# Two token-mixing stages: suffix sums that run on in one bank, score products in fours, values in pairs, another split of the PSUM banks and another order

## The reference, cut to what matters

```
proj = h @ w_in                       # 1024 -> 3072 columns: q, k, v of three kinds of heads
o_a  = chunk_band_attention(...)      # 6 band heads, 64 wide
o_b  = diff_attention(...)            # 4 differential heads: two softmax maps each, queries and keys 32 wide
o_c  = stick_breaking_attention(...)  # 6 stick-breaking heads, 64 wide
y    = concat(o_a, o_b, o_c) @ w_out
```

```
log_one_minus = where(strict, log_sigmoid(-z), 0)
suffix = cumsum(log_one_minus, reverse=True) - log_one_minus
a = where(strict, exp(log_beta + suffix), 0)
```

## Time and profile before

| | us |
|---|---|
| median of 3 runs | 2588.81 (2588.8 to 2589.32) |
| the profiled execution | 2589.32 |
| its span in the profile | 2587.5 |
| TensorE matmul busy | 2560.7 (99%) |
| VectorE, ScalarE, GpSimd busy | 1637.7, 1169.8, 423.3 |
| the `MIX_ORDER` part of the first mixing (981.8 to 1245.3) | 263.5 |
| granted TensorE clock | full in all slices but the first |

### The profile page before, as it was taken

How to read it: one execution, slowest core, us unless ns; L and a number is a source line. 1 busy time by engine, 2 the same in 40 slices (tenths; PEclk the granted TensorE clock), 3 DMA queues, 4 the chain that set the end, 5 groups by cost and what they waited for, 6 DMA issues and landing times.

```text
span 2587.5 us, 42242 instructions
## 1 busy us (share of the span) xinstructions
PE 2560.7 (99%) x17332; PEld 2222.2 (86%) x17332; DVE 1637.7 (63%) x2667; ACT 1169.8 (45%) x2019; POOL 423.3 (16%) x416
## 2 busy tenths in 40 slices
PE   9999999999999999999999999999999999999998
PEld 7788887678999888867899988999888876899987
DVE  3425653667999353456699735899444356699833
ACT  4123333643655234465455533555334456355522
POOL 0230010001332011111143200233001020133200
PEclk9999999999999999999999999999999999999999
DMA  8722140012333232211233332332323212223321
GB/s 323 290 93 93 38 123 33 34 58 82 99 106 107 98 117 67 66 50 66 82 115 100 113 114 66 115 115 98 114 82 104 64 50 83 66 90 115 115 96 67
DMA packets 183854, 252.73 MB, mean 98 GB/s; under 512 B 13040, under 2 KB 158448, under 8 KB 179184
## 3 DMA queue, kind: packets, MB, share of 16 engines
q1 hardware_dynamic: 183664, 250.04, 29.0%
HBM read 247.92 MB, written 2.10 MB: 97 GB/s over the span
## 4 chain that ended last, share of the span: by engine, by line
PE 92%; DVE 3%; ACT 2%; issue 1%; DMA 1%; POOL 1%; SPq 0%; POOLq 0%; ACTq 0%; DVEq 0%
PE psum L816 89%; PE psum L1384 1%; DMA mod_w<-in_l_ab_w_mod 1%; PE psum L1268 1%; PE psum L884 1%; DVE stats_first L2206 0%; DVE work L2199 0%; ACT w_hi L1558 0%; DVE X L2202 0%; ACT work L1606 0%; POOL stats_first L2925 0%; PE psum L860 0%; DVE h_lo L2138 0%; DVE wide L2236 0%; POOL stats L2980 0%
## 5 line engine op out<-in xcount | busy, mean ns | idle before, releaser
L816 PE MATMUL psum<-h_hi,w_hi 128*128 128x256 f32 (+1 forms) x1520 | 498.2, 328 | 0.4 <-DVE w_lo L2105 0.3
L816 PE MATMUL psum<-h_lo,w_hi 128*128 128x256 f32 (+1 forms) x1520 | 490.9, 323 | 0.0
L816 PE MATMUL psum<-h_hi,w_lo 128*128 128x256 f32 (+1 forms) x1520 | 490.8, 323 | 0.0
L2105 DVE TENSOR_TENSOR w_lo<-raw,w_hi 128x2048 fp32r<-128x2048 f32 (+1 forms) x99 | 223.4, 2260 | 295.1 <-ACT w_hi L1558 294.6
L816 PEld LDWEIGHTS psum<-h_hi,w_hi 128*128 128x128 f32 x1520 | 290.0, 191 | 32.6 <-issue 9.7
L816 PEld LDWEIGHTS psum<-h_hi,w_lo 128*128 128x128 f32 x1520 | 289.6, 191 | 22.6
L816 PEld LDWEIGHTS psum<-h_lo,w_hi 128*128 128x128 f32 x1520 | 289.9, 191 | 20.0 <-issue 0.5
L1558 ACT ACTIVATE w_hi<-raw 128x2048 fp32r<-128x2048 f32 (+1 forms) x100 | 188.5, 1888 | 259.5 <-PE psum L816 249.5
L816 PE MATMUL psum<-w_hi,ff_hi 128*128 128x512 f32 x576 | 225.2, 391 | 1.2 <-DVE ff_lo L2722 1.2
L816 PE MATMUL psum<-w_lo,ff_hi 128*128 128x512 f32 x576 | 224.4, 390 | 0.0
L816 PE MATMUL psum<-w_hi,ff_lo 128*128 128x512 f32 x576 | 224.4, 390 | 0.0
(11 more groups left out here) (364 smaller groups left out, 5444.4 us busy)
## 6 DMA issues: line engine op xcount, KB each, us to landing
raw<-in_ffn_w_gate SPq DMA_DIRECT2D x44, 1024.0 KB, 5.2
raw<-in_ffn_w_up SPq DMA_DIRECT2D x44, 1024.0 KB, 5.2
raw<-in_ffn_w_down SPq DMA_DIRECT2D x44, 1024.0 KB, 4.7
raw<-in_w_in SPq DMA_DIRECT2D x36, 512.0 KB, 5.0
raw<-in_l_ab_w_in SPq DMA_DIRECT2D x10, 1024.0 KB, 9.3
mod_w<-in_l_ab_w_mod SPq DMA_DIRECT2D x8, 1024.0 KB, 17.9
raw<-in_w_out SPq DMA_DIRECT2D x8, 1024.0 KB, 4.8
raw<-in_cd_w_in SPq DMA_DIRECT2D x7, 1024.0 KB, 5.3
```

What stands on the lines that cost most here:

```text
L816: return pe.matmul(o, lhsT, rhs, start=start, stop=stop, skip_group_check=True)
L2105: dve.tensor_tensor(lo[:, 0:nk * n], raw[c % 2][:, 0:nk * n], hi[:, 0:nk * n].bitcast(F32), ALU.subtract).then_inc(*w_lo_made.mark(key))
```

## The change

1. **Suffix sums.** The key tiles are taken from the last to the first, all of a head in one bank (`("csum", s, h)`). After tile `kt+1` has been read by VectorE, a product with `strict` (its sum with `suffix_tri` is all ones) completes that tile's columns to a full sum, and the triangle product of tile `kt` is added. So `stick_sums` has a product over `strict` (128, 256, 384 wide) in place of those over `ones`, and it waits for VectorE's step before.
2. **Scores of differential heads.** `diff_quad` makes the four maps of two heads one behind the other, at rows 0, 32, 64, 96, in four banks.
3. **Values.** `band_value_pair` and `diff_value_pair` make two heads' values in one bank, side by side.
4. **Banks.** Projections have bank 0 alone, band and differential heads 1 to 5, stick-breaking heads 6 and 7; `widen` comes late.
5. **Order.** All four strings are new.
6. **Feed-forward.** S3 and S4 move from GpSimd to VectorE (`last_mixed`), behind the rests of A1 and A22 and ahead of the other rests.

```diff
-    streams["a"] = [step for i in range(0, len(bands), 2) for step in [("band_pair", *streams["a"][i][1:]), *streams["a"][i:i + 2]]]
+    for letter, both in (("a", "band_pair"), ("c", "band_value_pair"), ("d", "diff_quad"), ("g", "diff_value_pair")):
+        single = streams[letter]
+        streams[letter] = [step for i in range(0, len(single), 2) for step in [(both, *single[i][1:]), *single[i:i + 2]]]
-                           [("stick_sums", h, kt) for kt in range(NT)] + ...
+                           [("stick_sums", h, kt) for kt in reversed(range(NT))] + ...
 MIX_LETTERS = {
-    "pe": ("vppspspsaapbpbppppappbbppppcpcappppppppppcbcppcppttbppssbpdtpptppdfppadpssppsppcpppbpspspsfbpccpppabppppcppdpbafbdpppppc"
-           "ssgttgttpffgdpcsspdpppcsdfspspspbbppgappppfdggfdppdfpfdgpgpppfcdggppfdgcstbfdbggastfdccttssfabbsccabbgnfgccbbpcpaogcppnp"
-           "pppppnbobppppppccooprpppnpppppppprppppr"),
+    "pe": ("pppappabpbpapppcbppppspbsppspapppppcbbppppbcpppbtapptspptppdspppppcpbpppfptppsppabppspppabppcspfbpspsdgspbbppapppppctp"
+           "pppfdtpfptgdspfpspsftpsppppsbfcgspdspsfbvppcgpdfpfppdapfttsgstfstsbbcafgnsbpbpafocppgabpbppnpdcopppbbppfpfnogcppppprpn"
+           "pppproppppppppr"),
...
-                proj, soft, stick = Ring([0, 1]), Ring([2, 3, 4]), Ring([5, 6, 7])
+                proj, soft, stick = Ring([0]), Ring([1, 2, 3, 4, 5]), Ring([6, 7])
...
+                    elif kind == "band_value_pair":
...
+                        for odd in range(2):
+                            pe.wait_ge(*probs_turned["a", s, i + odd])
+                            done(attend(v_a, h + odd, t, b, turned["a"][(i + odd) % 2]), ("av", s, i + odd))
...
+                    elif kind == "diff_quad":
...
+                        banks = [claim(soft.take(), ("bs", s, i + n // 2, n % 2)) for n in range(4)]
...
+                        for n, b in enumerate(banks):
+                            p0 = 32 * n
+                            done(mm(bank(b, width), q_b[p0:p0 + 32, h // 2, t * P:(t + 1) * P], k_b[p0:p0 + 32, h // 2, 0:width], True, True),
+                                 ("bs", s, i + n // 2, n % 2))
...
                     elif kind == "stick_sums":
...
-                        m = mm(bank(b, L - kt * P), tri[:, :], soft_[:, STARTS[kt]:STARTS[kt] + L - kt * P], True, kt == 3)
-                        for k2 in range(kt + 1, NT):
-                            m = mm(bank(b, L - k2 * P, (k2 - kt) * P), ones[:, :], soft_[:, STARTS[k2]:STARTS[k2] + L - k2 * P], False, k2 == 3)
+                        if kt == NT - 1:
+                            claim(stick.take(), ("csum", s, h))
...
+                        else:
+                            pe.wait_ge(*stick_dve["sums", s, h, kt + 1])
+                            mm(full(("csum", s, h), L - (kt + 1) * P, (kt + 1) * P), strict[:, 0, :], soft_[:, STARTS[kt + 1]:STARTS[kt + 1] + L - (kt + 1) * P],
+                               False, False)
+                        m = mm(full(("csum", s, h), L - kt * P, kt * P), tri[:, :], soft_[:, STARTS[kt]:STARTS[kt] + L - kt * P], kt == NT - 1, kt == 0)
...
                 first_mixed(keys[0])
                 for name in ("A1", "A22"):
                     lo_blocks(keys[0], name)
+                last_mixed(keys[0])
...
-                        for q, key in enumerate(fast_keys(s[1], layer)):
-                            mixed_ = {name: fast_weights(key, name)[2] for name in ("S1", "S2", "S3", "S4")}
...
-                            pool.tensor_tensor(mixed_["S3"], fast_block(key, 0, 0), fast_block(key, 0, 1), ALU.subtract).then_inc(*fast_mixed.mark((key, "S3")))
```

More of the change, by code:

```diff
@@ L189, in mix_streams @@
                            ([("stick_part", h, part) for part in range(3)] + [("stick_scores", h)]) * (letter == "s") + [("stick_abs", h), ("stick_log", h), ("stick_mask", h)] +
-                           [("stick_sums", h, kt) for kt in range(NT)] + [("stick_exp", h)] + [("stick_value_pair", h)] * (letter == "s") +
+                           [("stick_sums", h, kt) for kt in reversed(range(NT))] + [("stick_exp", h)] + [("stick_value_pair", h)] * (letter == "s") +
                            [("stick_values", h)]]
@@ L245 @@
 BAND_ITEM = {(step[2], step[3]): step[1] for step in MIX_ORDER["dve"] if step[0] == "band_scores"}
-DIFF_ITEM = {(step[2], step[3]): step[1] for step in MIX_ORDER["pe"] if step[0] == "diff_scores"}
+DIFF_ITEM = {(step[2], step[3]): step[1] for step in MIX_ORDER["dve"] if step[0] == "diff_scores"}
 def build(nc, A, out):
@@ L1433, in mixing @@
                         turn_probs(("at", s, i), band_slot(i), t)
-                    elif kind == "band_values":
+                    elif kind == "band_value_pair":
                         _, i, h, t = step
                         b = claim(soft.take(), ("av", s, i))
+                        bank_of["av", s, i + 1] = b
                         if h in (0, 4):
                             pe.wait_ge(*mix_kept[s, "v", int(h == 4), t])
-                        pe.wait_ge(*probs_turned["a", s, i])
-                        done(attend(v_a, h, t, b, turned["a"][i % 2]), ("av", s, i))
-                    elif kind == "diff_scores":
+                        for odd in range(2):
+                            pe.wait_ge(*probs_turned["a", s, i + odd])
+                            done(attend(v_a, h + odd, t, b, turned["a"][(i + odd) % 2]), ("av", s, i + odd))
+                    elif kind == "diff_quad":
                         _, i, h, t = step
                         width = (t + 1) * P
[L1444 to L1449, removed]
+                        banks = [claim(soft.take(), ("bs", s, i + n // 2, n % 2)) for n in range(4)]
+                        if t == 0:
+                            pe.wait_ge(*mix_kept[s, 1408 + P * (h // 2)])
+                        for n, b in enumerate(banks):
+                            p0 = 32 * n
+                            done(mm(bank(b, width), q_b[p0:p0 + 32, h // 2, t * P:(t + 1) * P], k_b[p0:p0 + 32, h // 2, 0:width], True, True),
+                                 ("bs", s, i + n // 2, n % 2))
                     elif kind == "diff_turn":
@@ L1453, in mixing @@
                         turn_probs(("bt", s, i), map0[i % 2], t)
-                    elif kind == "diff_values":
+                    elif kind == "diff_value_pair":
                         _, i, h, t = step
                         b = claim(soft.take(), ("bv", s, i))
+                        bank_of["bv", s, i + 1] = b
                         if h == 0:
                             pe.wait_ge(*mix_kept[s, "v", 3, t])
-                        pe.wait_ge(*probs_turned["b", s, i])
-                        done(attend(v_b, h, t, b, turned["b"][i % 2]), ("bv", s, i))
+                        for odd in range(2):
+                            pe.wait_ge(*probs_turned["b", s, i + odd])
+                            done(attend(v_b, h + odd, t, b, turned["b"][(i + odd) % 2]), ("bv", s, i + odd))
                     elif kind == "stick_part":
@@ L2037, in mixing @@
                         event = ("bv", s, i)
-                        copy(o_tok[:, t, 384 + h * 64:384 + (h + 1) * 64], event, full(event, 64), attn_kept, (s, i), scale=stat("diff", i, 6, 7))
+                        act.wait_ge(*psum_full["bv", s, i | 1])
+                        copy(o_tok[:, t, 384 + h * 64:384 + (h + 1) * 64], event, full(event, 64, 64 * (h % 2)), attn_kept, (s, i), scale=stat("diff", i, 6, 7))
+                        freed["bv", s, i - h % 2] = attn_kept[s, i]
                     elif kind == "stick_scores":
@@ L2056, in mixing @@
                         z = stick_ring[h % 2][1]
-                        act.wait_ge(*stick_dve["sums", s, h, 3])
+                        act.wait_ge(*stick_dve["sums", s, h, 0])
                         act.activation(z[:, :], z[:, :], ACT.Exp).then_inc(*stick_step.mark(("weights", s, h)))
@@ L2671, in first_mixed, with last_mixed @@
                     dve.tensor_tensor(s2, s1, fast_block(key, 0, 0), ALU.subtract).then_inc(*fast_first.mark((key, "S2")))
+                def last_mixed(key):
+                    s2, s3, s4 = (fast_weights(key, name)[2] for name in ("S2", "S3", "S4"))
+                    dve.tensor_tensor(s3, fast_block(key, 0, 0), fast_block(key, 0, 1), ALU.subtract).then_inc(*fast_mixed.mark((key, "S3")))
+                    dve.wait_ge(*fast_first[key, "S2"])
+                    dve.tensor_tensor(s4, fast_block(key, 1, 0), s2, ALU.subtract).then_inc(*fast_mixed.mark((key, "S4")))
                 def half_sums(q):
@@ L2748, in ffn @@
                         lo_blocks(following, "A22")
+                        last_mixed(following)
                     else:
```

42 lines of the change are left out of this document (17 added, 25 removed).

## The result

The changed kernel takes 2556.05 us (median of four runs, 2555.84 to 2556.28), the kernel before 2589.07 on the same chip. The ratio is 0.9872, 95% interval 0.9855 to 0.9889. The direction was right, and 13.8 us of gain were not foreseen (in the spans, 2554.5 us where the sum gave 2568.3).

What follows compares the result with a forecast made beforehand. TensorE, busy 99% of the span, was taken as the bound; 2587.5 - 25.2 (10.6 + 11.7 + 2.9) + 6.0 = 2568.3 us of span, 2569.6 us predicted time, range 2557 to 2583.

Steps and rivals of the forecast that it cites:

- Suffix sums: TensorE's stick-breaking sums in the mixings: `strict` replacing `ones` saves 0.88 us a head, 10.6 us in both layers.
- Quads: TensorE's differential scores: four maps in one step cost as much as two, saving 11.7 us in both layers.
- quads in twos: Rival for differential scores: third and fourth row groups wait, the 11.7 us gain falls away, 2581.3 us; chance 0.10.
- Feed-forward at nothing: Key loop: S3 and S4 add 1.2 us a key to VectorE, regained from GpSimd's absence; 0 us, bounds 0 and 5.
- The last rival: VectorE becomes the bound in feed-forward, 0.5 us over TensorE a key, 36 us, 2605.6 us; chance 0.03.
- New waits, +6 us: TensorE's waits in the mixings for the one projection bank and VectorE's subtractions: 3 us a layer; bounds minus 5, plus 20.
- The bank's 0.6: Waits at new projections' claims of the one bank, 27 a layer, with ScalarE free: 0.6 us a layer.
- The doubling: The sum of new waits doubled to 3 us a layer because ScalarE and VectorE aren't always free.
- Values: TensorE's value products in the mixings: 13 more neighbours a layer at 0.11 us, 2.9 us saved in both; bounds 1.6, 4.2.
- 53 to 55, nothing: Stretches of TensorE's dense work, each with a switch at both ends, go from 53 to 55, which costs nothing.
- The late chain: Rival: TensorE waits for a stick-breaking pair's scores-to-mask chain, 3 us at two pairs a layer, 12 us, 2581.6; chance 0.13.

Runs made afterwards that it cites:

- z2: The changed kernel with eight attention steps a layer, standing at claims of the projection bank, moved behind the next projection's first piece; 2574.31 us against 2556.22 unaltered.
- y1: The changed kernel with one additional full-array product between the two heads' products of each value pair, 40 in all; 2569.82 us.
- y2: The changed kernel with the same kind of additional full-array product ahead of each value pair, 40 in all; 2561.36 us.
- v3: The changed kernel with VectorE's split of chunk 10's weights moved behind two band scores, one step of band values and two of differential weights; 2555.88 us.
- y4_swap: The changed kernel with one exchange in TensorE's order, `(4, 3)` before `(5, 2)` at the end of heads 5 and 4; 2560.29 us against 2556.22 unaltered.

## Why the prediction fell short, by its own steps

- Suffix sums: right (10.6 forecast, 10.5 given back).
- Quads: right in sum (11.7; 11.6 to 11.8 by the distances, up to 12.8 by the time) and in the mechanism: 1.07 us for a quad of 512. The rival "quads in twos" fell, and had it been true it would have cost 6.7 us, not 11.7. The Trainium skill (TensorE: Matmul & The Clock Gate, Part 3: Packing small matmuls) has four row tiles at 3.07 times the speed of one after the other, and the prediction's estimate from it was 1.12 us. This trace nearly agrees: 1.07.
- Feed-forward at nothing: right, and for the stated reason, GpSimd's company. The last rival fell with it. VectorE's load didn't stay, as the prediction had it, but fell by 10 us in 194. (A key is 84 x 194.0/1566 = 10.4 us there and not 10.1; nothing hangs on it.)
- **New waits, +6 us: the step that failed.** The prediction let the 2.7 us of old idle time stand in each layer and added 3. The trace has 2.5 in all, so the term was -0.3: 6.3 of the 13.8 us. Two things were wrong in it. Of the 3 us, 1.9 came: 0.45 for `(5, 2)`, foreseen at 0.5, and 0.55, 0.62 and 0.23 for two late masks and a copy of scores, which the sum didn't have. The bank's 0.6, doubled, came to nothing: every claim had a cover longer than its copy, and eight bare ones cost 18 us (z2). The doubling had no row behind it. And of the old 2.7 some 2 us went with the new order, about 4 in both layers. That is the larger part; the range had it in its low end, the sum did not.
- **Values and "53 to 55, nothing": mis-sized.** I counted stretches of dense work, where the array's changes of shape had to be counted. In the two traces the entries from full-array products into small shapes fall from 52 to 38 in the first mixing. A change there and back costs 0.28 us (y1, y2), and the sum had the 0.10 of it that lies on the small step. The other 0.18, at 14 places in both layers, is 5.0 us that the sum left out. This is an estimate: no run undoes those entries alone, and the price of 64-column products is taken for scores as well.
- **A hidden wait in the kernel before.** Its last score pair 512 columns wide took 1.90 us, where the prediction priced it at 1.06. First TensorE (the pair, then a narrower window of it), then VectorE:
```profile
1174.50 1.98 PE L816 MATMUL psum<-k_b,q_b 32*128 32x512 f32 x4
1176.40 1.15 PE L816 MATMUL psum<-v_a,work 128*64 128x64 f32 x32
...
1175.35 1.12 PE L816 MATMUL psum<-k_b,q_b 32*128 32x512 f32 x2
```
```profile
1174.28 1.02 DVE L2874 TENSOR_TENSOR log_weights<-log_weights,psum 128x384 f32<-128x384 f32 x2 [2.18 <-PE psum L816]
```
By the old string the second map takes the bank of a suffix sum, which VectorE reads until 1175.30; the map starts at 1175.35 and runs behind the first instead of beside it. No idle time is recorded, since the first map was still running. The second mixing has the same at 2161.60. In the changed kernel no quad is longer than its usual time. That is 0.84 us a layer, 1.7 in both, in no term of the sum.
- The late chain, forecast as a rival of 12 us: it exists, at 0.55 and 0.62 us at two places a layer in the changed kernel, within the 2.5 us of idle.
- Still open: 13.8 - 6.3 - 5.0 - 1.7 = 0.8 us. Of these terms the 5.0 is an estimate, and the other two are read from traces of two kernels whose orders differ. No experiment divides them, and single parts of the change in the old order weren't tried.

## What to carry to other kernels

When one buffer replaces two, list for each claim what stands between the last use and the next, and compare it with the copy: if every cover is longer, as at the 27 claims here, no wait is left for a second buffer to save (no run gave the second bank back in the new order); but moving a few steps then costs a good part of the gain. Price a small-shaped product with the steps ahead of it and behind it, not only from its own start. Don't take the old idle time for a constant when the order changes, and look for waits in steps that are longer than their likes, not only in idle time. And look for the engine that ended 0.1 us before a wait's end before trusting the name on the wait.

## What the hardware showed that was not expected

- The granted clock of TensorE fell behind close waits. In the changed kernel 0.45 and 0.62 us of idle within 2.5 us left it at 1.00. In v3 the same pair (0.45 and 0.61) was followed by 0.66 over 2125 to 2130, at the second mixing only; in y4_swap one wait of 1.98 us was followed by 0.66 over 1155 to 1160. In such a stretch a pair of 128x256 sums took 0.86 us from start to start instead of 0.43: half speed, the lower level of 1.2 GHz, for some 3 us, which costs 1.4. Runs of one kernel differ by about this much (2554.69 to 2556.47 in v3), so a gain of 0.7 us a layer can be smaller than what it sets off.
- A 128x2048 operation of two inputs on VectorE holds up one small GpSimd operation for its whole length (2.50 us for 0.46). The reverse shows too: with GpSimd still, the 18 512-column operations of one line of VectorE went from 1.79 to 0.68 us, and taking over its work lowered VectorE's own load by 10 us in 194.
- Going from 64-column products to a full one and back costs TensorE 0.28 us beyond the products, and only 0.10 of it lies on the small step.
